# Norm sums by token columns, low-rank products side by side, and a merge moved among the pairs, in a two-layer hybrid block

## The reference, cut to what matters

```
x = rms_norm(x, g1) * (1 + scale) + shift            # shift, scale, gate: silu(c) @ w_ada, 12 groups per layer
p = x @ w_in                                         # A, B, C, D inputs and four gates
A: attention, 8 query heads over 2 key heads     B: attention with low-rank q and kv
D: attention with a bias of its neighbourhood    C: RWKV scan, forwards and backwards, in chunks of 64 tokens
   C per direction d: decay = f(w0[d] + tanh(w_lo_d) @ w_decay[d]);  a = sigmoid(a0[d] + a_lo_d @ w_aaa[d])
y = sum_i sigmoid(gate_i) * (out_i @ w_branch[i]);   x += gate1 * (y @ w_out)
x += gate2 * (relu(modulate(rms_norm(x, g2))) ... squared) @ w_mlp2
return rms_norm(x, g_final)
```

## Time and profile before

| | |
|---|---|
| Median of the runs | 2704.57 us |
| Profiled execution | 2709.78 us, span 2708.0 us |
| TensorE (PE) busy | 2571.4 us, 95% of the span |
| PE weight loads (PEld) | 1524.4 us |
| VectorE (DVE), ScalarE (ACT), GpSimd (POOL) | 793.0, 594.7, 233.3 us |
| PE's granted clock, mean | 0.983 |
| HBM read | 234.76 MB, 87 GB/s over the span |

### The profile page before, as it was taken

How to read it: one execution, slowest core, us unless ns; L and a number is a source line. 1 busy time by engine, 2 the same in 40 slices (tenths; PEclk the granted TensorE clock), 3 DMA queues, 4 the chain that set the end, 5 groups by cost and what they waited for, 6 DMA issues and landing times.

```text
span 2708.0 us, 51522 instructions
## 1 busy us (share of the span) xinstructions
PE 2571.4 (95%) x23352; PEld 1524.4 (56%) x23352; DVE 793.0 (29%) x1581; ACT 594.7 (22%) x1268; POOL 233.3 (9%) x244
## 2 busy tenths in 40 slices
PE   6999999999999999989999998999998998899998
PEld 3544654455555554444444445567756665678887
DVE  1552333343434422121100003441344444421101
ACT  2344323122223211020000002441223232211100
POOL 0000000122122300000000000000012232100000
PEclk9999999999999999999999999999999998999999
DMA  6201111232232334232222224122331111134453
GB/s 257 62 17 62 47 55 55 86 103 98 70 126 65 126 103 148 78 113 75 77 78 78 70 78 168 46 70 63 116 94 35 42 41 34 49 111 130 150 152 104
DMA packets 63882, 239.14 MB, mean 88 GB/s; under 512 B 6992, under 2 KB 8032, under 8 KB 62896
## 3 DMA queue, kind: packets, MB, share of 16 engines
q1 hardware_dynamic: 60768, 218.13, 25.7%
q0 software_dynamic: 2896, 17.71, 1.7%
HBM read 234.76 MB, written 1.05 MB: 87 GB/s over the span
## 4 chain that ended last, share of the span: by engine, by line
PE 58%; DVE 3%; ACT 2%; issue 1%; DMA 1%; DVEq 0%; SPq 0%; ACTq 0%
PE psum L419 57%; DVE arena L1563 1%; PE psum L658 1%; ACT arena L1505 1%; DMA panel_ring<-panels 1%; DVE arena L1133 0%; DVE arena L1136 0%; DVE arena L597 0%; DVE arena L797 0%; DVE arena L1324 0%; DVE arena L1317 0%; DVE normed L602 0%; ACT L1615 0%; ACT L901 0%; ACT arena L1113 0%
## 5 line engine op out<-in xcount | busy, mean ns | idle before, releaser
L419 PE MATMUL psum<-normed,panel_ring 128*128 128x512 f32 (+1 forms) x3136 | 1166.3, 518 | 14.5 <-ACT normed L620 13.0
L419 PEld LDWEIGHTS psum<-normed,panel_ring 128*128 128x128 f32 x3136 | 576.9, 192 | 448.3 <-issue 405.4
L419 PE MATMUL psum<-arena 64*64 64x64 f32 (+5 forms) x15256 | 586.4, 246 | 54.0 <-DVE arena L1563 18.4
L419 PE MATMUL psum<-arena,panel_ring 128*128 128x512 f32 (+1 forms) x1792 | 612.2, 493 | 1.8 <-ACT arena L1039 1.8
L419 PEld LDWEIGHTS psum<-arena 64*64 64x64 f32 (+3 forms) x15256 | 385.7, 138 | 340.8 <-issue 208.6
L419 PEld LDWEIGHTS psum<-arena,panel_ring 128*128 128x128 f32 x1792 | 334.6, 191 | 232.1 <-issue 206.7
L686 DVE TENSOR_REDUCE softmax_stats<-psum 128x1 f32<-128x512 f32 (+1 forms) x144 | 83.9, 600 | 170.5 <-PE psum L419 169.4
L711 ACT ACTIVATE arena<-psum,softmax_stats 128x512 f32<-128x512 f32 (+1 forms) x144 | 87.7, 613 | 206.7 <-DVE softmax_stats L686 123.6
L1768 DVE TENSOR_TENSOR arena<-arena 128x512 f32<-128x512 f32 (+1 forms) x64 | 35.8, 559 | 303.6 <-ACT arena L1755 303.6
L1654 DVE SCALAR_TENSOR_TENSOR arena<-psum,modulation,arena 128x256 f32<-128x256 f32 x24 | 10.9, 480 | 326.3 <-PE psum L419 326.3
L1537 POOL TENSOR_SCALAR arena<-arena 128x64 f32<-128x64 f32 x96 | 73.1, 775 | 333.1 <-DVE arena L1576 183.0
(11 more groups left out here) (148 smaller groups left out, 1416.9 us busy)
## 6 DMA issues: line engine op xcount, KB each, us to landing
panel_ring<-panels SPq DMA_DIRECT2D x398, 512.0 KB, 3.6
arena<-panels SPq DMA_DIRECT2D x16, 512.0 KB, 16.4
arena<-small_b POOLq DMA_DIRECT2D x2, 2176.0 KB, 9.9
arena<-x_t POOLq DMA_DIRECT2D x2, 2048.0 KB, 15.3
arena<-bias_d POOLq DMA_DIRECT2D x2, 2048.0 KB, 9.2
arena<-const_r POOLq DMA_DIRECT2D x2, 800.0 KB, 7.0
arena<-small_c POOLq DMA_DIRECT2D x2, 768.0 KB, 4.7
arena<-const_t POOLq DMA_DIRECT2D x2, 640.0 KB, 4.2
```

The costliest lines, as they stand in the source:

```text
L419: return nc.tensor.matmul(out, lhsT, rhs, start=start, stop=stop, skip_group_check=check)
```

## The change

Five things change.

1. A norm's sums. ScalarE's squares stay; VectorE adds tiles 0 to 6 into one (`add`, `acc`), and TensorE multiplies the sum and then tile 7 as the *stationary* operand with two columns of ones (`token_sums`), once for each 128 tokens: the sums lie with tokens on partitions, two columns for each 128 tokens. Root and reciprocal work on these 4 or 8 columns; TensorE spreads the result back over the partitions (a column, broadcast, times the identity), and `stage_scale` multiplies from PSUM. A root of a small operand at the head of `stage_out` and `stage_squares` draws the table load ahead.
2. x is loaded by the SP queue, in two halves, ahead of the early panels, and squared before group 0 of w_ada.
3. Groups of w_ada: layer 0's out norm has group 8, its MLP's norm 9, layer 1's out norm 10 and 11.
4. `prep`'s low-rank products go in twos, both directions in banks 2 and 3. In the scan the backward direction's sums move to bank 1, and their value products ahead of z's semaphore.
5. In layer 1, C's low-rank panels and the first pair's panels are D attention's filler, and merge A joins B and D among the pairs. The barrier of layer 1 goes, and the arena is laid out anew for it.

```diff
+    def token_sums(bank, src, n, first):
+        for tt in range(n // P):
+            p = mm(psum[:, bank, 2 * tt:2 * tt + 2], src[:, tt * P:(tt + 1) * P], ones[:, 0:2], first and tt == 0, not first, check=True)
+        return p
...
     def stage_scale(...):
         def act(e):
             e.wait_ge(sums_full.h, sums_full.at(1))
-            nc.scalar.activation(rstd[:, :n], psum[:, bank, :n], ACT.Sqrt, bias=eps, scale=1.0 / D_MODEL).then_inc(rooted.h, 1)
+            nc.scalar.activation(cols, psum[:, bank, :2 * n // P], ACT.Sqrt, bias=eps, scale=1.0 / D_MODEL).then_inc(rooted.h, 1)
...
+        def pe(e):
+            yield
+            e.wait_ge(inverted.h, inverted.at(1))
+            for tt in range(n // P):
+                p = mm(psum[:, bank, tt * P:(tt + 1) * P], norm_cols[:, 2 * tt:2 * tt + 1].broadcast_to([P, P]), ident, True, True)
+            p.then_inc(spread_out.h, 1)
...
     def stage_out(...):                       # stage_mlp likewise
-        def sum_of(e, k):
-            e.wait_ge(squared.h, squared.at(k + 1))
-            p = mm(psum[:, 6, :n], ones, h[:, k, tok], k == 0, k == KT - 1)
+        def sum_up(e):
+            e.wait_ge(added.h, added.at(KT - 2))
+            token_sums(6, acc[:, :n], n, True)
+            e.wait_ge(squared.h, squared.at(KT))
+            token_sums(6, h[:, KT - 1, tok], n, False).then_inc(sums_full.h, 1)
+        def add(e, k):
+            e.wait_ge(squared.h, squared.at(k + 1))
+            if k > 1:
+                e.wait_ge(added.h, added.at(k - 1))
+            nc.vector.tensor_tensor(acc[:, :n], h[:, 0, tok] if k == 1 else acc[:, :n], h[:, k, tok], ALU.add).then_inc(added.h, 1)
...
         def act(e):
+            nc.scalar.activation(norm_cols[:, 0:1], eps, ACT.Sqrt)
...
     prep_pe:
             for n, o in enumerate((SC_DEC, SC_AAA)):
+                if n == 0:
+                    e.wait_ge(s_root.h, s_root.at(1))
+                else:
+                    e.wait_ge(s_th.h, s_th.at(2))
                 for d in range(2):
-                    if n + d == 0:
-                        e.wait_ge(s_root.h, s_root.at(1))
-                    else:
-                        e.wait_ge(s_th.h, s_th.at(2 * n + d))
-                    mm(psum[:, 3, :], small[half[d], o + ft * P:o + (ft + 1) * P], lora[half[d], n, :],
+                    mm(psum[:, 2 + d, :], small[half[d], o + ft * P:o + (ft + 1) * P], lora[half[d], n, :],
                        True, True).then_inc(s_lo.h, 1)
-                    yield
+                yield
+                yield
...
     core_pe, the scan:
+                if 0 < i < NCH - 1:
+                    for hd in range(2):
+                        t, c = tside(1, hd), order[1][i]
+                        p = mm(sums[1][half[hd]], kt[t, 1, c, :], vt[t, 1, c, :], True, False, check=True)
                 p.then_inc(z_full.h, 1)
...
     the plan:
-    place(stage_ada(0, range(0, 2), ROW3, TURN3))
-    place(stage_squares("x", full_row, 0, start_sums))
-    place(stage_ada(0, range(2, 3), ROW3, TURN3))
-    stage, scaled = stage_scale("norm1_0", 0, full_row, 0, start_sums, rstd0)
+    place(stage_squares("x", rstd0, 0, start_sums))
+    first = stage_ada(0, range(0, 4), ROW3, TURN3)
+    place(first, 5)
+    stage, scaled = stage_scale("norm1_0", 0, full_row, 0, start_sums)
     place(stage)
-    place(stage_ada(0, range(3, 4), ROW3, TURN3))
+    place(first)
...
+        if l < DEPTH - 1:
             rest = [whole(merge)]
             weave(att, rest, [5] * att.steps)
             fill(rest, 1000)
             barrier()
+            ...
+        else:
+            rest = [whole(lora_stage), whole(first_stage)]
+            weave(att, rest, [3] * att.steps)
+            fill(rest, 1000)
+            attended = d_done
...
-        for i in (1, 3):
+        for i in (1, 3) if l < DEPTH - 1 else (0, 1, 3):
...
+        behind = late_groups([8] if l == 0 else [10, 11])
+        place(behind[0], 1)
+        norm, scaled = stage_scale(f"norm2_{l}", l, tok, 6, sums)
+        place(norm)
         for stage in behind:
-            place(stage, 4)
+            place(stage, 4 - stage.placed)
...
         @block.sync
+            for n in range(2):
+                eng.dma_start(x[:, 4 * n:4 * n + 4, :], x_t[4 * n * P:4 * (n + 1) * P, :].rearrange("(k p) t -> p k t", p=P)).then_inc(x_in[n].h, 16)
```

More of the change, by code:

```diff
@@ L453, in panel_tm @@
                     yield
[L455 removed]
+    c_in, small_in, x_in = sem("c_in"), sem("small_in"), [sem(f"x_in_{n}") for n in range(2)]
     mod_ready = sem("mod_ready")
@@ L576, in pe, with dve @@
         def pe(e):
-            for k in range(KT):
+            e.wait_ge(added.h, added.at(KT - 2))
+            token_sums(bank, acc, T, True)
+            e.wait_ge(squared.h, squared.at(KT))
+            token_sums(bank, h[:, KT - 1, :], T, False).then_inc(base.h, 1)
+            yield
+        def dve(e):
+            for k in range(1, KT - 1):
                 e.wait_ge(squared.h, squared.at(k + 1))
-                p = mm(psum[:, bank, :tok.stop - tok.start], ones, h[:, k, tok], k == 0, k == KT - 1)
@@ L1867, in layout @@
+        for begin, end, group in places:
+            take, _ = carver(begin, end)
+            for n in group:
+                at[n] = take(*names[n])
         take, _ = carver(one)
@@ L1917, in layer @@
                                  lambda t, i, qt: at["d_bias"][:, qt - 2, 2 * t + i, :], at["prob"], at["probT"], begin_d)
-        merge, _ = stage_branch(l, 0, tok, at["o_a"], at["y"], at["gate"], at["part"])
-        rest = [whole(merge)]
-        weave(att, rest, [5] * att.steps)
-        fill(rest, 1000)
-        barrier()
         rkv = lambda p: [at["c_rkv"][:, p % 2, n, :] for n in range(3)]
@@ L1926, in layer @@
         lora_panels = [(12 + n, at["c_lora"][:, n, :]) for n in range(3)]
-        stage, _, lora_ready = stage_c(l, at, lora_panels)
-        place(stage)
-        stage, n_z, _ = stage_c(l, at, panels_of(0))
-        place(stage)
+        merge, _ = stage_branch(l, 0, tok, at["o_a"], at["y"], at["gate"], at["part"])
+        lora_stage, _, lora_ready = stage_c(l, at, lora_panels, loadable=b_done)
+        first_stage, n_z, _ = stage_c(l, at, panels_of(0))
+        if l < DEPTH - 1:
+            rest = [whole(merge)]
+            weave(att, rest, [5] * att.steps)
+            fill(rest, 1000)
+            barrier()
+            place(lora_stage)
+            place(first_stage)
+            attended = None
+        else:
+            rest = [whole(lora_stage), whole(first_stage)]
+            weave(att, rest, [3] * att.steps)
+            fill(rest, 1000)
+            attended = d_done
         pairs, projected = [], [None]
@@ L1989, in layer @@
         if l == 0:
-            behind = [stage_ada(1, [g], ("row_" + "ab"[g % 2], [7 - 4 * (g % 2)]), ("turn_" + "ab"[g % 2], [7 - 4 * (g % 2)]))
-                      for g in (10, 11)]
-            for stage in behind:
-                place(stage, 4)
-            norm, scaled = stage_scale("norm1_1", 1, full_row, 6, sums, at["rstd"])
+            behind = late_groups([9])
+            place(behind[0], 1)
+            norm, scaled = stage_scale("norm1_1", 1, full_row, 6, sums)
             place(norm)
+            place(behind[0], 3)
             norm, ready = stage_modulate("norm1_1", 1, 0, full_row, scaled)
@@ L1998, in layer @@
             behind = []
-            norm, ready = stage_scale("final", l, tok, 6, sums, at["rstd"], final=True)
+            norm, ready = stage_scale("final", l, tok, 6, sums, final=True)
         place(norm)
```

159 lines of the change are left out of this document (86 added, 73 removed).

## The result

The changed kernel takes 2634.38 us (median of 4 runs, 2633.75 to 2641.69) beside 2705.94 for the one before (4 runs, 2700.43 to 2707.48): a ratio of 0.9748, interval 0.9729 to 0.9768. A second set of the same kernel gave 2636.49 (2635.41 to 2638.05), ratio 0.9752 (0.9735 to 0.9769).

What follows compares the result with a forecast made beforehand. TensorE, busy 2571.4 us of a 2708.0 span, was taken to bound the kernel. Terms summed to -55.2 us on 2709.8, giving 2654.6; with the median 5.2 lower, 2649.4, stated as 2650, range 2628 to 2674.

Steps and rivals of the forecast that it cites:

- 1 sums out of the loops: Merge and MLP output loops: six of eight products with ones leave each of four stages, additions hidden on VectorE; -15.5 us.
- 2 start: Kernel start: x ahead of the early panels, group 3's last panel becomes the limit, first modulation about 35; -12 us.
- 3 norm, out to MLP, layer 0: Layer 0's norm between out and MLP: only group 8 stands there, chain shorter, 1.5 given back for half clock; -6.6 us.
- 4 norm, MLP to layer 1: Norm between layer 0's MLP and layer 1: one group instead of two, A's first panel done at 1653.9; -7.8 us.
- 5 norm, out to MLP, layer 1: Layer 1's norm between out and MLP: groups 10 and 11 bring 8 panels for 6 slots, 7.3 us wait; +9.5 us.
- 6 last norm: The last norm: add, narrow sums, small root and reciprocal, spreading instead of a sum; -0.8 us.
- 7 products abreast: Low-rank products in the pairs: both directions back to back, 16 visits of 1.06 us remain of 32; -15 us.
- 8 merge A and C's panels, layer 1: Layer 1: merge A as filler fills idle in the pairs, -12 us; C's panels slow D attention, +5 us.
- the exchange gains nothing: Rival, layer 1: VectorE holds up D attention (+12), idle in the pairs shrinks by only 5; 2664 us, chance 0.17.
- products not overlapping: Rival, low-rank products: each still takes its own 0.86 us, saving 0 to 3; 2663 us, chance 0.05.
- the clock rival: Rival: denser fillers end half-clock stretches in layer 1's pairs (15 us), the start runs warm (3 us); 2632 us, chance 0.14.
- The two rules: Trainium skill: PSUM sources cost scalings 2.6 us, a 1380 ns drain makes each preload worth 2.7; forecast followed the trace instead.

## Why the prediction was nearly right, step by step

| Part | predicted | traces of before and after | shown by undoing it |
|---|---|---|---|
| 1 sums out of the loops | -15.5 | -13.1 | 14.2 |
| 2 start | -12 | -11.5 | 11.9 |
| 3 norm, out to MLP, layer 0 | -6.6 | -6.1 | |
| 4 norm, MLP to layer 1 | -7.8 | -5.5 | |
| 5 norm, out to MLP, layer 1 | +9.5 | +5.5 | |
| 6 last norm | -0.8 | -0.3 | |
| 7 products abreast | -15 | | 14.7 |
| 8 merge A and C's panels, layer 1 | -12 + 5 | | 10.8 |
| Sum | -55.2 | | -56.5 |

The sum takes 14.7 and 10.8 from the experiments, since in the traces of before and after the pairs' numbers have the clock in them. What is left of the 68.1 is 11.6 us, nearly all of it in layer 1's D attention and pairs (27.0 moved, where the experiments give 15.1), and the 20.5 us at half clock in before's profile account for 10.2 of them (half of 20.5).

**1.** Right, product for product, but for the place: in each out stage the sixth product lies behind the last residual, so between first and last residual an out stage lost five of them (an MLP six). The traces' 13.1 has 1.3 us of groups 10 and 11 in it, which end inside layer 1's MLP now. **7.** Right: side by side, two products take the time of one, and 14.7 to 17 of the 17 us so saved come back when it is undone.

**2.** Right in size, and in this profile for the reason given (group 3's last panel ends it, 31.99 for a predicted 30.9); in four of nine profiles the work itself ends it, at about the same time. The queue's part in it was not seen.

**3, 4.** The chain of small products took longer than forecast. I had last residual to modulation at 6.1 and 5.9 us; it is 7.8 in layer 0 (1151.62 to 1159.40) and 7.9 behind the MLP (1602.37 to 1610.32). The granted clock is 0.50 from 1155 to 1161 with TensorE busy throughout, behind 1.57 us of idle; the spreading products take 2.08 us there and 0.71 for half as many in layer 1, where the clock stayed at 1.00 between 2394 and 2398. I had set 1.5 aside for this in part 3 and nothing in part 4. That it is the clock and not the chain's own length, three other executions show behind the MLP: with the same instructions and the same 1.57 us of idle the clock stayed at 1.00, and the chain took 6.05 us. TensorE's rows there in the kernel with the products one by one:

```profile
1612.16 1.05 PE L420 MATMUL psum<-const_global,arena 128*128 128x2 f32 x8 [1.57 <-DVE arena L1773]
1613.07 1.03 PE L420 MATMUL psum<-const_global,normed 128*128 128x2 f32 x8
1614.04 0.65 PE L420 MATMUL psum<-panel_ring,c_silu_wide 128*32 128x128 f32 x16
1614.70 1.16 PE L420 MATMUL psum<-const_global,norm_cols 128*128 128x128 f32 x8
```

The whole norm took 14.8 us in those three, for 16.7 in after: 7.4 less than the 22.25 of before, where the forecast had 7.8. The term's sum was right at full clock; the half clock was the step left out.

**5.** Too dear by 4.0, and most of it in my picture of before. From the last residual to the first relu I forecast 18.9 us (2465.3 to 2484.2); it takes 18.05 (2393.21 to 2411.26), with the wait at 6.34 for 7.3 (7.0 in the second set). But before needed 12.5 for it, not the 9.5 that I had read from the modulation's end: behind 4.12 us of idle a part of its first MLP panels ran at the lower clock, which this row of before's PE timeline has (37 records in 11.19 us, where 64 take 14.04 at full clock; the clock from 2466 to 2478 was 0.72):

```profile
2471.05 11.19 PE L419 MATMUL psum<-normed,panel_ring 128*128 128x256 f32 x37 [4.12 <-ACT normed L620]
```

The two groups also cost 1.3 us inside layer 1's MLP (218.8 us from its first relu to its last residual in after, 217.6 in the kernel with the groups back), so the exchange cost 6.8 in all.

**8.** Beside part 5 the term most off in size. Net -10.8 for a predicted -7 (13 against the median of the other profiles' pairs): the pairs gave 13.6 where I had 12, and D attention cost 1.8 where I had 5. The reckoning of gaps itself was not tested, only its outcome; a merge takes 41.1 us by itself, for the forecast's 42 (3.72/16, its row, is 0.23 and not 0.22, but 64 such records take 14.04, which is 0.22 each). VectorE does run C's steps between head steps, but from D attention's first exponential to the first root of a `prep` TensorE idles 1.3 us of 66.8 (1.2 of 106.1 before), so it doesn't wait for them. That rival (the exchange gains nothing) is out, and so is that of products not overlapping.

**The clock.** 16 us lie between the forecast and the median, and the sum has only 1.3 of them. The result is nearer to the clock rival's 2632 (chance 0.14) than to my own 2650. The rival's mechanism as stated is half right: layer 1's pairs have one stretch of 3.4 us at half clock where the profile of before had 20.5 and three of 3.4, but both kernels with the merge put back lost the long one too. What holds over all runs is the mean: 0.983 before (25 runs), 0.991 after (8 runs). At 1.3 to 1.6 us for each 0.001 that is 10 to 13 us, most of the missing amount, if the relation within one kernel holds between two. No single part carries it: with the merge back it is 0.989, with the groups back 0.989, with the start back 0.990; and without the early root, which hardly changes TensorE's work, it is 0.989 as well, so 0.002 says little. Part of it is counted in terms 2 and 3 already, where half-clock products went. Why the other part of it comes about stays open.

**The two rules.** On the PSUM operand the trace of after agrees with that of before. VectorE's groups by form (busy, mean ns): scalings that read the factor from PSUM, and additions that read SBUF alone.

```profile
L632 DVE TENSOR_TENSOR normed<-arena,psum 128x512 f32<-128x512 f32 x24 | 14.6, 681 | 6.3 <-PE psum L420 6.3
...
L1710 DVE TENSOR_TENSOR arena<-arena,normed 128x512 f32<-128x512 f32 x5 | 3.4, 680 | 0.0
```

681 and 680 ns: the 62 cycles that the Trainium skill (VectorE: DVE Perf Modes, the TRN2 errata) puts between them don't show. The Trainium skill's drain of 1380 ns (ScalarE: Activation LUTs, What ACT_TABLE_LOAD costs) doesn't show either. In the kernel without the early root the load starts at 2390.73, 0.01 us behind the last square's end, takes 1.28 us, and the root starts at 2392.03, 0.02 us behind the load. With the drain two such loads would be 5.3 us of ScalarE's time; what they held the roots up by is 0.3 us in layer 1 and nothing in layer 0, since a load passes beside the sums on TensorE.

## What to carry to other kernels

Cost a move by the product's own stream time and by the gaps it lands in, place for place: here five of eight such terms came within 1.5 us of what one profile or one experiment shows. Count what stands in a ring of slots behind each pause: the seventh and eighth panel cost 6 to 9 us at whichever norm they stood, and up to about 3 once put among work. Where small products follow a short idle, cost them at both clocks: the same chain took 6.05 us at full clock and 7.9 where the clock fell, and which it is changed from one execution to the next. And read one profile against several before a difference of 3 us is believed.

## What the runs showed that I had not expected

- 1.57 us of idle behind a long full stretch was followed by 6 us at a granted clock of 0.50 with TensorE busy all through (1155 to 1161); behind 0.91 us of idle in layer 1 the clock stayed at 1.00 (2394 to 2398). Behind the MLP the same instructions with the same 1.57 us of idle were at half clock in some executions (6.8 us of it in after) and at full clock in three others.
- The same kernel's runs on one chip differ by up to 16 us (the kernel before, 2695.8 to 2711.4), and go with their mean granted clock (0.978 and 2711.5 us, 0.987 and 2698.3), more than most single parts of this change are worth.
- The same 2 MB of x on another queue beside the same panels let TensorE begin 7.5 to 7.7 us later.
